# A chain of two transformer blocks on one NeuronCore: attention's output projection in three fp32r terms, two ada sums ahead of the norm, four rotary swaps on ACT

## What is computed

```python
cond = jax.nn.silu(c)                               # c: (1, 1024)
mod = cond @ ada_w[l] + ada_b[l]                    # shift, scale, gate of layer l
h = rms_norm(x, norm_g[l]) * (1 + scale) + shift
z = h @ even_w_in[0]                                # layer 0, width 7296
...
q, k, v, qi, ki, wi, g = split_cols(h @ odd_w_in[0])   # layer 1
q = rope(q); k = rope(k)                            # 16 heads of 128, one key head
qi = rope(qi); ki = rope(ki)                        # 8 index heads of 64, one index key
o = dsa_attention(q, k, v, qi, ki, wi, positions)   # 64 keys per query, chosen by the index scores
x = x + gate * ((o * silu(g)) @ odd_w_out[0])       # (256, 2048) @ (2048, 1024)
```

## Time and profile before

| | us |
|---|---|
| median of 3 runs | 2081.6 (2076.55 to 2081.71) |
| profiled execution | 2082.09 |
| its span | 2080.4 |
| PE, DVE, ACT busy | 1971.0, 1405.2, 970.7 |

### The profile page before, as it was taken

How to read it: one execution, slowest core, us unless ns; L and a number is a source line. 1 busy time by engine, 2 the same in 40 slices (tenths; PEclk the granted TensorE clock), 3 DMA queues, 4 the chain that set the end, 5 groups by cost and what they waited for, 6 DMA issues and landing times. The chain is left out here.

```text
span 2080.4 us, 29539 instructions
## 1 busy us (share of the span) xinstructions
PE 1971.0 (95%) x12399; PEld 1780.2 (86%) x12399; DVE 1405.2 (68%) x1704; ACT 970.7 (47%) x1107; POOL 80.1 (4%) x123
## 2 busy tenths in 40 slices
PE   3988899998999999999999899999999999999998
PEld 3867788887878868899999799999898989898976
DVE  5788798353764045666546578787878888888862
ACT  2411111223364112443445567666676666666654
POOL 3000000000000010100121000000000000000000
PEclk7999899998999999999999999999999999999999
DMA  9744321445152342356753468999898999898980
GB/s 308 265 140 139 104 83 37 147 137 188 42 202 82 122 150 75 103 183 193 191 213 132 140 242 331 346 332 350 325 353 325 349 331 352 329 349 327 348 311 21
DMA packets 225855, 452.27 MB, mean 217 GB/s; under 512 B 6944, under 2 KB 91176, under 8 KB 225720
## 3 DMA queue, kind: packets, MB, share of 16 engines
q1 hardware_dynamic: 222400, 445.44, 61.0%
q0 software_dynamic: 1632, 4.75, 0.9%
q10 hardware_dynamic: 1688, 0.15, 0.1%
HBM read 448.21 MB, written 2.10 MB: 216 GB/s over the span
## 5 line engine op out<-in xcount | busy, mean ns | idle before, releaser
L1926 DVE TENSOR_TENSOR ring_r<-ring,his_r 128x2816 fp32r<-128x2816 f32 (+1 forms) x192 | 587.2, 3085 | 62.4 <-ACT his_r L1481 62.3
L1481 ACT ACTIVATE his_r<-ring 128x2816 fp32r<-128x2816 f32 (+1 forms) x192 | 491.2, 2560 | 199.2 <-DMA ring<-in_moe_w_dram 191.1
L1122 PE MATMUL bank<-his_r,hg_r 128*128 128x352 f32 x2048 | 356.4, 326 | 0.8 <-ACT hg_r L1505 0.8
L1122 PEld LDWEIGHTS bank<-his_r,hg_r 128*128 128x128 f32 x2048 | 334.0, 188 | 1.8 <-issue 0.9
L2398 PE MATMUL bank<-hT,ring 128*128 128x256 f32 x912 | 215.5, 393 | 3.9 <-DVE arena L2973 2.1
L2398 PEld LDWEIGHTS bank<-hT,ring 128*128 128x128 f32 x912 | 175.6, 196 | 32.5 <-issue 7.9
L1122 PE MATMUL bank<-ring_r,hg_r 128*128 128x352 f32 x1024 | 185.9, 323 | 0.0
L1122 PEld LDWEIGHTS bank<-ring_r,hg_r 128*128 128x128 f32 x1024 | 169.0, 188 | 0.0
L2176 PE MATMUL bank<-arena,ring 128*128 128x256 f32 x480 | 106.2, 380 | 1.8 <-ACT cw L1406 0.7
L2176 PEld LDWEIGHTS bank<-arena,ring 128*128 128x128 f32 x480 | 91.0, 190 | 15.1 <-ACT cw L1406 1.0
L2994 DVE SCALAR_TENSOR_TENSOR arena<-ring,cw,arena 128x256 f32<-128x256 f32 x240 | 96.5, 476 | 0.1
(11 more groups left out here) (534 smaller groups left out, 2825.9 us busy)
## 6 DMA issues: line engine op xcount, KB each, us to landing
ring<-in_moe_w_dram SPq DMA_DIRECT2D x128, 1408.0 KB, 8.4
ring<-in_moe_w_dram SPq DMA_DIRECT2D x48, 1536.0 KB, 8.9
ring<-in_even_w_in_dram SPq DMA_DIRECT2D x28, 1024.0 KB, 5.8
ring<-in_ffn_w_dram SPq DMA_DIRECT2D x22, 1024.0 KB, 5.3
ring<-in_ada_w_dram SPq DMA_DIRECT2D x20, 1024.0 KB, 8.0
ring<-in_odd_w_in_dram SPq DMA_DIRECT2D x9, 2048.0 KB, 7.8
ring<-in_moe_w_dram SPq DMA_DIRECT2D x16, 1024.0 KB, 7.2
ring<-in_a_w_in_dram SPq DMA_DIRECT2D x6, 2048.0 KB, 8.0
```

The lines of the kernel that those rows point to most:

```text
L1122: ins = mm(bank[first + m][:, 0:WC], x[:, KT // 2 * late + k, :], w[:, k, WC * m:WC * m + WC], start=(not late and k == 0 and s == "hg_hi" ...
L1481: A(moe_hi(n), moe_w(n), ACT.Copy).then_inc(sem("moe_hi"), 1)
L1926: V.tensor_tensor(moe_lo(n), moe_w(n), moe_hi(n).bitcast(F32), ALU.subtract).then_inc(sem("moe_lo"), 1)
```

## The change

Four things. (1) In the opening PE waits for `ones` alone, sums groups 0 and 1 before the norm tiles, and asks for the rest of the constants before z; DVE asks for them just before it makes scale and shift. (2) `rot(0, 2)` and `rot(2, 4)` leave PE; ACT's `swap_small` exchanges the halves of entries 0 to 3 by 14 copies. (3) The output projection is done in three terms: ACT's `gated_hi`, `oo_cast` and DVE's `gated_lo`, `oo_low` make the parts, in and behind the attention loop and beside the projection, with three buffers `ob_r` for the high part of a weight tile. (4) `SQ3` moves to free memory.

```diff
@@ -133,6 +133,8 @@
         cu_r = [sb_r("cu_hi_r", 21504, KT, T)[:, :, :], sb_r("cu_lo_r", 4096, KT, T)[:, :, :]]
+        gt_r = [sb_r("gt_hi_r", 0, 2 * KT, T)[:, :, :], sb_r("gt_lo_r", 4096, 2 * KT, T)[:, :, :]]
+        ob_r = [sb_r(f"ob_r{n}", off, 2 * KT, P)[:, :, :] for n, off in enumerate((11776, 21504, 19456))]
         at_lo_r = sb_r("at_lo_r", 9984, FT, SLOTS)
@@ -481,11 +483,11 @@
         ROUNDS = (2 * T - 1) // (SLOTS + 1)
-        MADE = {"ident": 1, "const": 2, "cmask": 3, "spatial": 4, "moe": 5}
+        MADE = {"ident": 1, "ones": 2, "const": 3, "cmask": 4, "spatial": 5, "moe": 6}
         SET = {"angles": 1, "gains": 2, "lam": 3}
...
         OT = reg(0, TT, D)
-        SQ3 = reg(0, KT, T)
+        SQ3 = reg(25088, KT, T)
         NSQ += [SQ2, SQ2, SQ2, reg(5632, KT, T)] + [SQ2] * 5
@@ -520,6 +522,21 @@
             return phases["cin"]["t0"] + 2 * u + 2
+
+        OO_HI = ["x0", "x1", "x2", "x3", "x4", "w0", "x5", "w1", "x6", "x7"] + [f"w{q}" for q in range(2, 8)]
+        OO_LO = ["x0", "x1", "x2", "x3", "x4", "w0", "x5", "x6", "x7"] + [f"w{q}" for q in range(1, 8)]
+
+        def oo_hi(name):
+
+            return sem("q_hi"), 9 + OO_HI.index(name) + 1
+
+        def oo_lo(name):
+
+            return sem("q_lo"), 9 + OO_LO.index(name) + 1
+
+        def oo_tile(q, flat=ring_flat):
+
+            return view(phases["oo"], q // 2, flat)[:, :, P * (q % 2):P * (q % 2) + P]
@@ -695,12 +712,7 @@
             def beside_q(q):
-                if q == 0:
-                    pe.wait_ge(*took("m2", 4))
-                    rot(0, 2)
-                elif q == 1:
-                    rot(2, 4)
-                elif 3 <= q < 11:
+                if 3 <= q < 11:
                     index(2 * (q - 3))
@@ -799,7 +811,22 @@
-            pe_gemm("oo", lambda k: GT[:, k, :], [(sem("o_taken"), 16)], between=norm_pair)
+            pe.wait_ge(sem("o_taken"), 16)
+            for q in range(8):
+                hi, lo = ob_r[q % 3], oo_tile(q, ring_r_flat)
+                if q >= 4:
+                    pe.wait_ge(*took("oo", q - 3))
+                pe.wait_ge(*oo_hi(f"w{q}"))
+                for w, x in ((hi, 0), (lo, 0), (hi, 1)):
+                    if w is lo:
+                        pe.wait_ge(*oo_lo(f"w{q}"))
+                    for k in range(2 * KT):
+                        if q == 0 and w is hi:
+                            pe.wait_ge(*(oo_lo(f"x{k // 2}") if x else oo_hi(f"x{k // 2}")))
+                        ins = mm(bank[q % 4][:, 0:T], w[:, k, :], gt_r[x][:, k, :], start=(w is hi and x == 0 and k == 0),
+                                 stop=(x == 1 and k == 2 * KT - 1))
+                ins.then_inc(acc_ready, 1)
+                norm_pair(q)
@@ -1273,8 +1300,24 @@
             take_gemm(act, "m2", take_m2)
+
+            def swap_small(i):
+                src, table, n = ROTS[i]
+                half = 32 if table == 1 else 64
+                if i >= 2:
+                    act.wait_ge(sem("rot_done"), i - 1)
+                for lo in range(0, P, half):
+                    other = lo ^ half
+                    ins = A(SWP[lo:lo + half, i % 2, 0:n, :], src()[other:other + half], ACT.Copy)
+                ins.then_inc(sem("swapped"), 1)
+
+            act.wait_ge(*took("m2", 4))
+            swap_small(0)
             q_cast(1)
+            swap_small(1)
             q_cast(2)
+            swap_small(2)
+            swap_small(3)
             def index(n):
@@ -1309,11 +1352,25 @@
+            def oo_cast(q):
+                wait_chunk(act, "oo", q // 2, 0)
+                if q >= 3:
+                    act.wait_ge(acc_ready, phases["oo"]["t0"] + q - 2)
+                A(ob_r[q % 3], oo_tile(q), ACT.Copy).then_inc(sem("q_hi"), 1)
+
+            def gated_hi(j):
+                act.wait_ge(sem("o_taken"), 2 * j + 2)
+                A(gt_r[0][:, 2 * j:2 * j + 2, :], GT[:, 2 * j:2 * j + 2, :], ACT.Copy).then_inc(sem("q_hi"), 1)
+
             def beside_attention(b):
...
                     gate_tile(2 + b)
+                if b >= 4 and b % 2 == 0:
+                    gated_hi(b // 2 - 2)
+                elif b >= 13:
+                    oo_cast((b - 13) // 2)
@@ -1334,9 +1391,14 @@
             attend(0, 16, 2, 6, 2 * T, beside_attention)
+            gated_hi(6)
+            gated_hi(7)
+            oo_cast(2)
             act.wait_ge(sem("dve_made"), SET["gains"])
...
                 act.wait_ge(*took("oo", q + 1))
+                if q < 5:
+                    oo_cast(q + 3)
                 A(hT[:, q, :], xT[:, q, :], ACT.Identity, scale=gs[:, q:q + 1]).then_inc(sem("xg_ready"), 1)
@@ -1601,7 +1663,7 @@
                         dve.wait_ge(sem("rot_done"), i - 1)
-                    turned = SWP[:, i % 2, 0:n, :] if 4 <= i < 12 else bank[5 + i % 2][:, 0:n * T].rearrange("p (n t) -> p n t", n=n)
+                    turned = SWP[:, i % 2, 0:n, :] if i < 12 else bank[5 + i % 2][:, 0:n * T].rearrange("p (n t) -> p n t", n=n)
                     ch(V.tensor_tensor(SWP[:, i % 2, 0:n, :], turned,
@@ -1689,16 +1751,31 @@
+            def gated_lo(j):
+                dve.wait_ge(*oo_hi(f"x{j}"))
+                r = slice(2 * j, 2 * j + 2)
+                V.tensor_tensor(gt_r[1][:, r, :], GT[:, r, :], gt_r[0][:, r, :].bitcast(F32), ALU.subtract).then_inc(sem("q_lo"), 1)
+
+            def oo_low(q):
+                dve.wait_ge(*oo_hi(f"w{q}"))
+                V.tensor_tensor(oo_tile(q, ring_r_flat), oo_tile(q), ob_r[q % 3].bitcast(F32), ALU.subtract).then_inc(sem("q_lo"), 1)
+
             def turn_later(b):
...
                     rotate(6 + b // 2, 7 + b // 2)
+                if b >= 5 and b % 2 == 1:
+                    gated_lo((b - 5) // 2)
+                elif b == 14:
+                    oo_low(0)
...
             V.tensor_scalar(SUBG, subln, 1.0 - LAM0, None, ALU.mult).then_inc(sem("dve_made"), 1)
+            gated_lo(7)
+            oo_low(1)
             take_gemm(dve, "oo", lambda q, lin, b: V.scalar_tensor_tensor(
-                xT[:, q, :], b, mod[:, 1, 16 + q:17 + q], xT[:, q, :], ALU.mult, ALU.add))
+                xT[:, q, :], b, mod[:, 1, 16 + q:17 + q], xT[:, q, :], ALU.mult, ALU.add), between=lambda q: oo_low(q + 2) if q < 6 else None)
             dve.wait_ge(sem("norm_rooted"), 3)
@@ -2294,7 +2371,8 @@
             pool.wait_ge(sem("pool_made"), MADE["ident"])
-            step(pool.memset(ones[:, :], 1.0))
+            pool.memset(ones[:, :], 1.0).then_inc(sem("pool_made"), 1)
+            pool.wait_ge(sem("pool_made"), MADE["ones"])
             for m in (swap_a, swap_i, swap_d, hsel, bmask):
@@ -2372,7 +2450,7 @@
             tr(bank[5][:, 380:504], CROW[0:124, 1, :], ident[0:124, 0:124]).then_inc(sem("turned_in"), 1)
-            pe.wait_ge(sem("pool_made"), MADE["const"])
+            pe.wait_ge(sem("pool_made"), MADE["ones"])
@@ -2544,11 +2622,14 @@
+            pe.wait_ge(sem("x_taken"), 3)
+            ada(0)
+            ada(1)
             for q in range(KT):
                 norm_tile(0, q)
-            pe.wait_ge(sem("x_taken"), 3)
-            for c in range(4):
-                ada(c)
+            ada(2)
+            ada(3)
+            pe.wait_ge(sem("pool_made"), MADE["const"])
             z("zL", 0, ready=lambda k: (sem("h_ready"), k + 1))
@@ -2951,7 +3032,6 @@
                 ada(j // 2, j % 2)
-            dve.wait_ge(sem("pool_made"), MADE["const"])
             ada(2, 0)
@@ -2962,6 +3042,7 @@
             ada(3, 1)
+            dve.wait_ge(sem("pool_made"), MADE["const"])
             modulation(0, 0, 16)
```

## The result

The changed kernel takes **2064.8 us** (median of 4 runs, 2063.9 to 2065.9) against 2079.7 of the kernel before (4 runs, 2076.6 to 2081.7): ratio 0.9929, 95% interval 0.9914 to 0.9943, so 12 to 18 us saved. The forecast was 2067.5, the range 2060 to 2075.

A forecast was written before the change was run, and what follows sets the result against it. The prediction took PE to set the pace, behind a POOL, PE norm, PE sums, DVE chain in the opening. Terms -9.2 - 2.4 + 6.6 - 9.1 = -14.1 us from the median 2081.6 gave 2067.5 us, range 2060 to 2075.

The forecast's parts named there:

- Opening, -9.2: Opening: sums before the norm, waiting only for ones, restart DVE and start z 9.2 us earlier.
- Rival C: Opening bound by loads: the 9.2 us are given back after 36 us; -4.9, 2076.7 us; chance 0.10.
- Swaps, -2.4: Query projection: PE loses four swap matmuls, ACT's 14 copies stay hidden; 2.4 us saved.
- the bound of 2.6: Query projection: up to 2.6 us saved by the swaps, counting the drawn-out record after each.
- Attention loop, 0: Attention loop: the added gated_hi and gated_lo copies fit ACT's and DVE's idle time; 0 us.
- Rival D: Attention loop: side work not covered, as scores, exponentials and weights form one chain; +6.5, 2074.0 us; chance 0.08.
- End of attention, +6.6: End of attention: uncovered cast and low part delay the projection 3.3 us, half clock adds 2.3 and 1.0; +6.6 us.
- the +1.0 for the first tile: Output projection's start: the first tile's first two or so us lose half to the 1.2 GHz clock; +1.0 us.
- The sign that the forecast named: Output projection's start: PE at half clock, with an idle gap over 3 us shortly before.
- Rival B: End of attention: PE's clock stays up, so the term is +3.3 and the time 2064.2 us; chance 0.20.
- Output projection, -9.1: Output projection: three terms take 5.76 us per tile instead of 6.90, over eight tiles; -9.1 us.
- The estimate of 13.8 us: Output projection: by four passes against one, three terms cost 3/4, saving 13.8 us; the forecast kept 9.1.

The follow-up runs named there:

- norm first: Changed kernel with the norm sum put back in front of the modulation sums, own mark for ones kept: 2067.5 us, ratio 0.9943 to the kernel before.
- late mark: Changed kernel with PE again waiting for all of POOL's constants before the first sums, new order kept: 2068.0 us, ratio 0.9940 to the kernel before.
- the projection alone: Kernel before with only the three-term output projection added, side work in the attention loop included: 2078.0 us, ratio 0.9989.
- first pair of traces: First profiled executions of the kernel before and the changed kernel: 2082.1 and 2063.9 us, spans 18.2 us apart.
- second pair: Both kernels profiled again, unchanged: medians 2079.0 us for the kernel before and 2065.0 for the changed one; spans 15.8 us apart.

## Why the prediction was right, and where its sizes were off

The time came out 2.7 us below the forecast. Of these 1.9 are the starting point: the forecast began at 2081.6, the median of three runs, and over four the kernel before has 2079.7. The gain is 15.0 us (12 to 18) where the sum said 14.1. Its mechanism is the forecast's in each term but for the clock of the projection's first tile; that the sum fits so closely is in part luck, for by the traces the opening was worth some 1.6 us less than said, and the end of the attention, the swaps and the projection together 1.6 more.

- **Opening, -9.2.** The chain was right (POOL, norm, sums, DVE), and the times at which DVE restarts and z begins are those named. But the term took one execution's 31.55 for the kernel before. The five traces with the old opening restart DVE at 31.55, 31.21, 30.46, 29.71 and 29.58 us, the seven with the new one at 22.04, 22.05 and five times 23.2 to 23.4 (norm first and late mark left aside), so the part is worth 6.2 to 9.5 us, 7.6 in the mean; the times say 5.9 (4 to 9). What varies is when POOL starts its last constant (22.9 to 23.8 us with the old opening) and when the clock is down: the first two sums of the new one took 1.85 or 2.06 us in two traces and 3.42 in five. Rival C fell: no load is waited for.
- **Swaps, -2.4.** Measured -2.9 and -2.8 in the traces, 0.2 to 0.3 beyond the bound of 2.6, which counted the drawn-out record behind each pair; where the rest comes from is open. The 14 copies took 7.6 us (7.4 estimated) and hid.
- **Attention loop, 0.** Holds in every trace, even with a cast and a low part more in it. Rival D is out.
- **End of attention, +6.6.** The step that was mis-sized, by 1.0: the waits cost 3.0 us (3.3 said), the half clock over the results 2.4 (2.3 said), but not the +1.0 for the first tile. The sign that the forecast named, half clock when the projection starts, did not come: in both traces of the changed kernel the clock was back at 0.85 to 0.90 in the us in which the tile began and at 1.00 behind it, and in the first of them the tile took 667.28 - 661.43 = 5.85 us, 0.09 more than the next; with the projection alone it took 1.7 more. So the term is 5.6 or 7.2, by when the clock comes back, and what decides that isn't settled. Rival B, clock kept, was wrong: its 2064.2 is near the measured time by the sizes of other terms. The Trainium skill's rule on idle gaps in mid-kernel (TensorE: Matmul & The Clock Gate, "Why this matters for your kernels") says that idle stretches of PE in mid-kernel put it back to half rate. The trace agrees here: 3.38 us idle, and 0.50 from 655 us on. Behind the equal gaps of 2.77 us near 760 us the traces show both, half clock in seven and full clock in five.
- **Output projection, -9.1.** Measured -9.2 in both pairs, and 1.92 us per term and tile when one was taken away. The estimate of 13.8 us from FP8 and Floating Point Precision, "TensorE Precision Notes" in the Trainium skill, is too high by 4.6. The page gives the four passes; that the reduced form needs one is the forecast's reading of it. Measured, true FP32 cost 6.90 us per tile against 1.92 for a term, a factor of 3.6 and not four.
- **Not in the sum.** -2.8 and -2.9 behind the wait near 760 us, and +1.2 near 1185 us, where both kernels are at half clock and the changed one gets it back some 2.5 us later (32 records of 128x128 in 6.67 us against 5.48). Nothing in the change touches these places. Of the 3.2 us between the first pair of traces (18.2) and the medians (15.0), the second pair (15.8) takes 2.4 away, nearly all in the first 212 us.

## What to carry to other kernels

A split into high and low parts that pays for itself in matmul time still needs its first cast and its first low part before the first matmul, and where these are placed decides: two instructions of 1.9 and 2.3 us put in front of the last softmax steps took back 5.6 of 9.2 us, and gave them all back when they were moved two blocks forward into idle time of the same engines. An idle gap of PE should be priced with the clock that may be lost behind it: 3.38 us of wait cost 2.4 us more at half clock. Real work brought forward into a gap of 2.77 us brought 4.3 and 5.5 us between traces of that stretch, 4.7 and 4.2 in the medians, whose intervals don't exclude the bare gap. A term that rests on one execution's opening, where engines wait for POOL and the clock moves, needs a second execution beside it before it is written down to a tenth.

## What the runs showed of the hardware

- One and the same norm sum (16 records of 128x256 fp32) took 3.62 us in one execution, with the granted clock at 1.00, and 5.1 to 5.5 or 6.2 to 6.7 in the thirteen others, with the clock at 0.50 in part or all of it, whether or not a wait for POOL of 1.8 to 2.9 us stood in front.
- Behind equal gaps of 2.77 us the granted clock stayed at 1.00, or fell to 0.50 for a time that cost 1.7 or 2.8 us. A gap of 1.59 us at the end of the attention left it at 1.00 where the next gap was 0.5 us or less; where one of 1.91 us followed behind 1.1 us of work, it fell to 0.50.
- ACT's copies between partitions went by columns alone: 32 and 64 partitions of 512 columns took 0.64 and 0.63 us, 32 and 64 of 256 columns 0.42 each.
